# Two tables of routed sums instead of one in a mixture-of-experts stage on Trainium2

## The reference

```python
    x = x + gt1 * rmsnorm(mixed @ w_out[l], g_post_mix[l])
    h2 = modulate(rmsnorm(x, g_pre_ffn[l]), sh2, sc2)
    # moe: 8 of 64 experts per token, each swiglu(h, wg, wu, wd) of width 256
    routed = jax.ops.segment_sum(y_blocks.reshape(n_pad, d), tok_buf, num_segments=t + 1)[:t]
    y = routed + swiglu(h, w_sg, w_su, w_sd)
    x = x + gt2 * rmsnorm(y, g_post_ffn[l])
```

## Time and profile before

| | us |
|---|---|
| median of 3 runs | 2325.89 (2323.56 to 2327.89) |
| the profiled execution: its own time | 2333.98 |
| the profiled execution: span from first to last instruction | 2332.3 |
| attention, its first DMA | at 372.05 |
| experts, from the first to the last scatter | 1231.4 to 2271.5 |
| final | 2285.4 to 2332.3 |

### The profile page before, as it was taken

The page is one execution under the profiler, slowest core; times in us unless marked ns, Lnnn a source line. Parts: engine busy times, 40 slices in busy tenths (PEclk is TensorE's granted clock), DMA queues, the critical chain, the costliest instruction groups (busy, mean ns, idle before and its releaser), DMA issues. The chain is left out here.

```text
span 2332.3 us, 35734 instructions
## 1 busy us (share of the span) xinstructions
PE 2035.9 (87%) x9400; PEld 1452.3 (62%) x9401; DVE 1432.4 (61%) x2085; ACT 1278.9 (55%) x2004; POOL 869.0 (37%) x876
## 2 busy tenths in 40 slices
PE   4999995889888887899839999999999999999980
PEld 2776673655555554666427777777766777777760
DVE  3751564663358433455537777777676777777773
ACT  2421122556666565222127777776766777777761
POOL 1010103631155110044434455555444545544561
PEclk8999997899999998999969999999999999999995
DMA  6464436411221111343289998789999888789736
GB/s 248 140 190 118 130 115 187 114 32 39 44 48 39 39 35 63 133 92 101 56 255 293 317 336 247 231 233 328 336 330 331 260 232 229 203 258 334 202 61 233
DMA packets 284779, 420.25 MB, mean 180 GB/s; under 512 B 27233, under 2 KB 213345, under 8 KB 284689
## 3 DMA queue, kind: packets, MB, share of 16 engines
q1 hardware_dynamic: 213314, 281.25, 35.2%
q0 software_dynamic: 60496, 116.37, 22.6%
q10 hardware_dynamic: 10896, 21.71, 3.0%
HBM read 352.51 MB, written 91.54 MB: 190 GB/s over the span
## 5 line engine op out<-in xcount | busy, mean ns | idle before, releaser
L1802 DVE TENSOR_TENSOR w_gate_up_low<-w_gate_up,w_gate_up_high 128x1024 fp32r<-128x1024 f32 x318 | 378.2, 1217 | 15.9 <-ACT w_gate_up_high L1747 15.9
L1831 DVE TENSOR_TENSOR w_down_low<-w_down,w_down_high 128x2048 fp32r<-128x2048 f32 x104 | 238.4, 2292 | 161.5 <-ACT w_down_high L1771 161.5
L1747 ACT ACTIVATE w_gate_up_high<-w_gate_up 128x1024 fp32r x318 | 312.1, 1047 | 39.4 <-issue 28.6
L935 DVE TENSOR_REDUCE neg_max<-ps_scores 128x1 f32<-128x1280 f32 x128 | 190.3, 1490 | 223.6 <-PE ps_scores L1020 223.2
L1876 PE MATMUL ps_gu<-w_gate_up_high,gatheredT_high 128*128 128x512 f32 x630 | 256.1, 407 | 2.7 <-DVE gatheredT_low L1810 1.4
L1878 PE MATMUL ps_gu<-w_gate_up_high,gatheredT_low 128*128 128x512 f32 x630 | 248.7, 395 | 0.0
L1877 PE MATMUL ps_gu<-w_gate_up_low,gatheredT_high 128*128 128x512 f32 x630 | 248.6, 395 | 0.0
L1695 POOL DMA_INDIRECT gathered<-h_scratch,e_gather_index x108 | 195.6, 1811 | 96.5 <-POOL e_gather_index L1692 91.2
L1709 POOL DMA_INDIRECT y_scratch<-e_y,e_target_index x104 | 182.5, 1754 | 95.3 <-ACT e_y L1784 39.0
L1771 ACT ACTIVATE w_down_high<-w_down 128x2048 fp32r x104 | 199.6, 1919 | 29.2 <-issue 28.0
L1020 PE MATMUL ps_scores<-k_high_low,q_high 128*128 128x512 f32 (+1 forms) x384 | 167.5, 436 | 47.0 <-ACT probs L895 18.9
(11 more groups left out here) (257 smaller groups left out, 4328.9 us busy)
## 6 DMA issues: line engine op xcount, KB each, us to landing
w_gate_up<-in_w_exp_gate SPq DMA_DIRECT2D x64, 1024.0 KB, 10.4
w_gate_up<-in_w_exp_up SPq DMA_DIRECT2D x64, 1024.0 KB, 13.9
w_down<-in_w_exp_down SPq DMA_DIRECT2D x64, 1024.0 KB, 15.5
w_mod_later<-in_w_mod ACTq DMA_DIRECT2D x32, 512.0 KB, 3.8
w_mod_first<-in_w_mod SPq DMA_DIRECT2D x4, 2048.0 KB, 15.6
w_in_raw<-in_w_in SPq DMA_DIRECT2D x32, 256.0 KB, 3.9
k_high_low<-k_scratch POOLq DMA_DIRECT2D x10, 640.0 KB, 8.0
values<-in_tokens SPq DMA_DIRECT2D x10, 512.0 KB, 11.3
```

Source lines behind the costliest of these rows:

```text
L935: nc.vector.tensor_reduce(nm[:, n % 4:n % 4 + 1], S[:, span(u, r)], AX.X, ALU.max, negate=True).then_inc(s_m, 1)
L1747: act.activation(wH[:, 2 * j:2 * j + 2], wgu[:, ds(slot, 1), 2 * j:2 * j + 2].rearrange("p o k n -> p (o k) n"), ACT.Copy).then_inc(S["wH" ...
L1802: nc.vector.tensor_tensor(wL[:, 2 * j:2 * j + 2], wgu[:, ds(slot, 1), 2 * j:2 * j + 2].rearrange("p o k n -> p (o k) n"), wH[:, 2 * j:2 * ...
L1831: nc.vector.tensor_tensor(dl[:], wdn[:, ds(slot, 1)].rearrange("p o k n -> p (o k) n"), dh[:].bitcast(F32), ALU.subtract).then_inc(S["dl"], 1)
```

## The change

A second table of the same size is made, so that `y_d` is a list of two. Table 0 gets the shared expert's rows and the scatters of even blocks, table 1 those of odd blocks. The second table's 1024 token rows are filled with zeros by one DMA of 4 MB from DRAM to DRAM, which SP issues at the start of `attention` between two small loads. Each table's pad rows are zeroed by a DMA of 512 KB (before: two of 256 KB for the one table).

`scat` becomes two semaphores, one for each parity. POOL's wait ahead of the target copy and ACT's wait ahead of the refill both ask that the scatter two blocks ago, the last one on the same table, has landed.

In `final` ACT also loads table 1 (two DMAs of 2 MB, issued ahead of the 4 MB of residual rows), and DVE adds its tiles to those of table 0: two before its wait for the residual rows, the other six between the operations of its loop. ACT's squares wait for these sums. To have enough semaphores, `final` uses those of the expert weights again, from the value that they have reached.

```diff
@@ attention, SP
             sp.dma_start(slot_d, a["k_pads"]).then_inc(s_later, 16)
+            sp.dma_start(y2_d[0:SEQ, :], a["k_zeros"]).then_inc(s_later, 16)
             sp.dma_start(first_row[:], a["k_first"].broadcast_to([P, E])).then_inc(s_later, 16)
             sp.dma_start(token[:], a["k_token"]).then_inc(s_later, 16)
             sp.wait_ge(s_q[1], 64)
@@ output_and_router, SP
-                    sp.dma_start(y_d[(t - 2) * P:(t - 1) * P, :], yb[:]).then_inc(s_ys, 16)
+                    sp.dma_start(y_d[0][(t - 2) * P:(t - 1) * P, :], yb[:]).then_inc(s_ys, 16)
@@ experts
+        s_scat = [b.sem(ph, f"e_scattered{u}") for u in range(2)]
@@ experts, POOL, block n
-                pool.wait_ge(S["scat"], n * 16 + 32)
+                pool.wait_ge(s_scat[u], i * 16 + 16)
                 pool.sem_inc(S["carry"], 1)
                 nc.gpsimd.tensor_copy(si[u][:], ir[:, ds(n & (RING - 1), 1)]).then_inc(S["target"], 1)
-
+                pool.wait_ge(S["target"], n + 1)
                 pool.wait_ge(S["y"], n * 2 + 4)
-                pool.wait_ge(S["target"], n + 1)
                 pool.sem_inc(S["carry"], 1)
-                pool.indirect_dma_start(y_d, bass.IndirectOffsetOnAxis(ap=si[u][:, 0:1], axis=0), yb[u][:], None,
-                                        bounds_check=SEQ + P - 1, compute_op=ALU.add).then_inc(S["scat"], 16)
+                pool.indirect_dma_start(y_d[u], bass.IndirectOffsetOnAxis(ap=si[u][:, 0:1], axis=0), yb[u][:], None,
+                                        bounds_check=SEQ + P - 1, compute_op=ALU.add).then_inc(s_scat[u], 16)
@@ experts, POOL, before the loop
-            for h in range(2):
-                pool.dma_start(y_d[SEQ + h * HD:SEQ + (h + 1) * HD, :], zero[0:HD]).then_inc(S["scat"], 16)
+            for u in range(2):
+                pool.dma_start(y_d[u][SEQ:SEQ + P, :], zero[:]).then_inc(s_scat[u], 16)
@@ experts, ACT, block n
-                act.wait_ge(S["scat"], n * 16 + 16)
+                act.wait_ge(s_scat[u], i * 16 + 16)
@@ final, ACT
+            for h in range(2):
+                act.dma_start(y2[:, 4 * h:4 * h + 4], y_d[1][4 * h * P:(4 * h + 4) * P, :].rearrange("(t p) n -> p t n", p=P)).then_inc(s_y2[h], 16)
             act.dma_start(xt[:], x1_d.rearrange("(t p) n -> p t n", p=P)).then_inc(s_x, 16)
             for t in range(NT):
-                act.wait_ge(s_y[t // 2], 16)
+                act.wait_ge(s_sum, t + 1)
@@ final, DVE
+            def joined(t):
+                dve.wait_ge(s_y[t // 2], y_base[t // 2] + 16)
+                dve.wait_ge(s_y2[t // 4], 16)
+                nc.vector.tensor_tensor(yt[:, t], yt[:, t], y2[:, t], ALU.add).then_inc(s_sum, 1)
+
+            joined(0)
+            joined(1)
             dve.wait_ge(s_x, 32)
             for t in range(NT):
+                if t + 2 < NT:
+                    joined(t + 2)
                 dve.wait_ge(s_rs, 2 * t + 2)
```

More of the change, by code:

```diff
@@ L677, in _, with attention @@
                     mod_products(wl[:, i % 2], h * QK, QK, h < 2, h >= 2, s_mm)
-def attention(b, a, ident, rows, nlam, mhalf, moe, wa, vv, q_d, k_d, o_d, rows_d, slot_d):
+def attention(b, a, ident, rows, nlam, mhalf, moe, wa, vv, q_d, k_d, o_d, rows_d, slot_d, y2_d):
     nc = b.nc
@@ L813, in _ @@
             store(NU - 1)
-            sp.wait_ge(s_later, 80)
+            sp.wait_ge(s_later, 96)
             sp.wait_ge(s_before, 16)
@@ L1641, in experts @@
             "xT", "xH", "xL", "wH", "wL", "wused", "gu", "silu", "act", "aTp", "aH", "dh", "dl",
-            "dn", "y", "weight", "rows", "target", "scat", "landed", "carry", "zeroed")}
+            "dn", "y", "weight", "rows", "target", "landed", "carry", "zeroed")}
         s_gather = [b.sem(ph, f"e_gathered{u}") for u in range(2)]
+        s_scat = [b.sem(ph, f"e_scattered{u}") for u in range(2)]
         s_index = [b.sem(ph, f"e_index_loaded{u}") for u in range(2)]
@@ L1734, in _ @@
                 pool.wait_ge(s_index[u], turns * 16 + 48)
-            pool.wait_ge(S["scat"], turns * 32 + 32)
+            for u in range(2):
+                pool.wait_ge(s_scat[u], turns * 16 + 16)
         @block.scalar
@@ L1915, in _, with final @@
             blocks(pe, body)
-def final(b, a, rows_d, mhalf, x1_d, y_d, out):
+def final(b, a, rows_d, mhalf, s_w, x1_d, y_d, out):
     nc = b.nc
@@ L1923, in final @@
         xt = b.sb(ph, "x1_tiles", [P, NT, D])
+        y2 = b.sb(ph, "y_tiles_odd", [P, NT, D])
         g2 = b.sb(ph, "gain_row", [P, D])
@@ L1926, in final @@
         ms = b.sb(ph, "f_mean", [P, 3, NT])
-        s_y = [b.sem(ph, f"y_loaded{h}") for h in range(NT // 2)]
+        s_y = s_w[0:NT // 2]
+        y_base = [(E - h + WS - 1) // WS * 48 for h in range(NT // 2)]
         s_x = b.sem(ph, "x1_loaded")
+        s_y2 = [b.sem(ph, f"y_odd_loaded{h}") for h in range(2)]
+        s_sum = b.sem(ph, "f_sum")
         s_sq = b.sem(ph, "f_sq")
@@ L1938, in _ @@
             for h in range(NT // 2):
-                sp.dma_start(yt[:, 2 * h:2 * h + 2], y_d[2 * h * P:(2 * h + 2) * P, :].rearrange("(t p) n -> p t n", p=P)).then_inc(s_y[h], 16)
+                sp.dma_start(yt[:, 2 * h:2 * h + 2], y_d[0][2 * h * P:(2 * h + 2) * P, :].rearrange("(t p) n -> p t n", p=P)).then_inc(s_y[h], 16)
             for t in range(NT):
@@ L1983, in program @@
     h2_d = nc.dram_tensor("h2_scratch", [SEQ, D + E], F32).ap()
-    y_d = nc.dram_tensor("y_scratch", [SEQ + P, D], F32).ap()
+    y_d = [nc.dram_tensor(f"y_scratch{u}", [SEQ + P, D], F32).ap() for u in range(2)]
     rows_d = nc.dram_tensor("rows_scratch", [1, 4 * D], F32).ap()
@@ L1995, in program @@
         s_slots = [b.sem(top, f"slots_stored{u}") for u in range(2)]
+        s_w = [b.sem(top, f"e_weights_loaded{u}") for u in range(WS)]
         with ExitStack() as kv:
@@ L2002, in program @@
             wa = b.sb(kv, "w_out_ahead", [P, AHEAD, D])
-            attention(b, a, ident, rows, nlam, mhalf, moe, wa, vv, q_d, k_d, o_d, rows_d, slot_d)
+            attention(b, a, ident, rows, nlam, mhalf, moe, wa, vv, q_d, k_d, o_d, rows_d, slot_d, y_d[1])
             output_and_router(b, a, ident, rows, mhalf, moe, wa, p8, s_slots, o_d, x1_d, h2_d, y_d, slot_d)
@@ L2008, in program @@
             wdn = b.sb(ex, "w_down", [P, WS, 2, D])
-            s_w = [b.sem(ex, f"e_weights_loaded{u}") for u in range(WS)]
             routing_tables(b, a, ident, mask, total, tab, wgu, wdn, s_w, p8, token, s_slots, slot_d)
             experts(b, a, ident, tab, wgu, wdn, s_w, s_slots, h2_d, y_d, slot_d)
-        final(b, a, rows_d, mhalf, x1_d, y_d, out)
+        final(b, a, rows_d, mhalf, s_w, x1_d, y_d, out)
 def rope_table():
@@ L2042 @@
     host["k_steps"] = np.arange(WS, E, WS, dtype=np.float32)[None, :(E - 1) // WS]
+    host["k_zeros"] = np.zeros((SEQ, D), np.float32)
     host["k_first"] = (np.arange(E, dtype=np.float32) * SEQ + 1)[None, :]
```

## The result

Twelve runs of each kernel side by side gave 2332.59 us for the changed one (2326.18 to 2339.39) and 2326.61 us for the one before (2318.79 to 2330.63). The ratio is 1.0029, with a 95% interval of 1.0016 to 1.0043: 6.7 us slower, between 3.7 and 10.0 (the medians themselves lie 6.0 apart). A second call, in the experiments, gave 1.0014 (1.0001 to 1.0026), that is 3.3 us (5.8 between the medians). I had forecast 3.9 us less. The kernel moved the other way, if only by 0.1 to 0.3%. One run of the whole study, 2456.97 us in the last experiment at a granted clock of 0.83 instead of 0.96, was in a slower state and is left out of every median.

A forecast was written before the change was run, and what follows sets the result against it. PE, busy 87% of the span, was taken as the bound, held up in the loop by a closed chain of scatters. Terms -27.9 - 0.8 + 7.4 + 17.4 = -3.9 us took 2325.9 to 2322.0 us; range 2310 to 2336.

The forecast's parts named there:

- loop, first to last silu: Experts' loop: waiting for the scatter two blocks back gives 27.9 us of the 39.1 lost above 9.70 per block.
- gap behind the last silu: Loop's end: the last target copy no longer waits 0.80 us for a landing scatter, 0.8 us less.
- zeros at attention's start: Attention's start: the 4.19 MB fill shares the engines with K and Q half and half, delaying everything by 7.4 us.
- end: Final stage: residual rows land 10.0 us later behind table 1, and six additions take 7.4 us; 17.4 in all.
- the fill goes first: Attention's start: a bound on the zeros' cost, with the fill served ahead of K and Q at 419 GB/s, 10.0 us.
- my own signs of being wrong: ACT waits for weights early, third window returns most of 14 us, scatter over 13 us, or fill's cost at either bound.
- rival (b): Loop: two scatters in flight make weights late; third and fourth window give nothing, +9.2 us, 2335.1 us; chance 0.12.
- third window: Loop stretch of one-block experts, bound by DMA at 1.03: of 14.0 us lost, 2.8 come back; bounds 0 and 14.0.
- fourth window: Loop stretch followed by experts of three and four blocks, whose loads aren't needed soon: all 10.3 us lost are gained.
- rival (d): Loop: scatter latency grows past 13 us and the wait returns; half the gain gone, +10.1 us, 2336.0 us; chance 0.08.
- (a): Loop: all waits go, weights' lead and DMA engines suffice; 39.1 us gained, sum -15.1, 2310.8 us; chance 0.15.
- Rival (c): Attention's start: zeros hidden, or cost 10 or 20 us; 2314.6, 2324.6 or 2334.6 us; chance hidden 0.08, at 20 us 0.07.

The follow-up runs named there:

- the last experiment: The kernel before, with one table, its residual rows loaded in four parts so that DVE starts with the first pair; 2320.93 us, ratio 0.9967.

## Why the prediction was wrong

The sum, term by term; measured is the difference of the means over all profiles with and without the part in question:

| term | forecast | measured |
|---|---|---|
| loop, first to last silu | -27.9 | -25.0 (1023.9 of seven, 1048.9 of six) |
| gap behind the last silu | -0.8 | -0.7 (20.7 of eight, 21.4 of six; it wanders by 1.6) |
| zeros at attention's start | +7.4 | +12.1 (24.67 of three, 12.54 of ten) |
| end | +17.4 | +16.9 (10.1 + 6.8) |
| sum | -3.9 | +3.3 |

3.3 us lies in the interval of the second comparison (0.2 to 6.0) and just under that of the first (3.7 to 10.0). The runs of the parts by themselves, each beside the kernel before, give -24.9 for the loop, +13.5 for the end and +10.5 for the fill, -0.9 together. From their three intervals I estimate some 9 us either way for that sum, so it contradicts nothing and is too coarse to confirm; the sum rests on the stages.

**The step that failed is the fill's: "if both queues get half of the engines, that takes about 7.4 us more".** It is the term +7.4, and it measured 12.1. The place was right, and that the fill takes the engines from K and Q; how they share was not. I shared time by queues. The engines shared it by turns, packet for packet (50 against 52), and a packet of the fill was 64 KB where one of K and Q was 1.7 KB. The fill in 2 KB pieces shows that this is the cause: 62.1% for K and Q instead of 10.8%, and 2.5 us instead of 12.1. The fill even came out 2 us above my bound of 10.0 for "the fill goes first". That bound took the rate of 419 GB/s from the earlier trace rows; the 64 packets of the fill needed 13.05 us for their 4.19 MB, which is 321 GB/s. Why this copy inside DRAM ran slower stays open; a reading and a writing of each byte in full, my 20.0, it was not. The 4.7 us of this term take the sum of -3.9 past zero. That the fill's cost comes out at a bound was one of my own signs of being wrong.

Here the Trainium skill (DMA: Bandwidth & Descriptors, Queues, rings and completion order) would have done better than I did. It says that a DMA engine takes its queues in turn and finishes a whole packet before it goes on to the next. I had set it aside under rival (b) because of q0's 0.5% of the earlier trace rows. At attention's start the trace agrees with it, with 50 packets of q1 and 52 of q0 side by side. And I misread: the scatter issued at 1698.38 has its first packet of row data at 1703.38, 5.0 us later, and the window ends ahead of that. From 1703 to 1708 us of the kernel before both queues move:

```profile
q0 software_dynamic: 193, 0.60, 56.7%
q1 hardware_dynamic: 318, 0.88, 47.9%
```

So the 0.5% showed a scatter that hadn't begun, not one that weights kept out. Why it begins 5.0 us behind its issue under weight loads, and 2.25 us behind it without them (the one at 2225.04), stays open.

**The loop fell 2.9 us short, and the windows came out otherwise than forecast.** What they lose above 9.70 us for a block, as means over the six profiles without the change and the seven with it, cut at the same blocks:

| window of the earlier trace rows | without | with | gain | forecast |
|---|---|---|---|---|
| first | 8.4 (7.3 to 10.0) | 0.0 | 8.4 | 8.5 |
| second | 1.9 (0.6 to 3.4) | 0.0 | 1.9 | 3.3 |
| third | 15.8 (14.0 to 16.9) | 13.3 (12.2 to 14.4) | 2.5 | 2.8 |
| fourth | 7.4 (5.5 to 10.3) | 1.6 (0.2 to 3.3) | 5.9 | 10.3 |
| fifth | 6.3 (3.0 to 8.3) | 0.0 | 6.3 | 3.0 |

The third window gave its 2.8 almost, although the first pair of profiles shows 0.5. The term that was too large is the fourth window's. I took its 10.3 from the one execution in which it lost most, and 1.6 of what it loses stays with the change; the fifth, at 3.0 the least of six, made good for some of it.

In the third window I had read the bound correctly: the DMA share stayed at 1.03 and the first idle time is ACT's ahead of the weight copy. In the profiled execution what I had counted as slack, the 4.3 us by which the weights were early at the window's end, is gone by its eighth block. ACT in that stretch, then SP:

```profile
1634.21 2.96 ACT L1749 ACTIVATE w_gate_up_high<-w_gate_up 128x1024 fp32r x3 [2.09 <-SPq L1665]
...
1647.86 2.95 ACT L1749 ACTIVATE w_gate_up_high<-w_gate_up 128x1024 fp32r x3 [6.22 <-SPq L1665]
```

```profile
1634.70 3.13 SPq L1516 DMA_DIRECT2D w_gate_up<-in_w_exp_gate  x1
1637.88 5.98 SPq L1517 DMA_DIRECT2D w_gate_up<-in_w_exp_up  x1
1643.90 3.70 SPq L1518 DMA_DIRECT2D w_down<-in_w_exp_down  x1
```

ACT starts 0.26 us after SP's third issue ends at 1647.60, which looks like a matter of order. But these weights had landed only at 1646.85, 0.75 us earlier, and the kernel with the earlier signal gained nothing in sum; the lighter loads confirmed capacity. With two thirds of a window at 9.70 and the rest in a few stalls of 2 to 6 us, the sum over seventeen blocks is still the DMA engines' time. In the profiled execution the loop gained 27.0, of which 1.6 are the first block's and not the change's. Over seven executions it is 25.0; in the slowest of them the dense blocks lost 17.8 us.

**What held.** A closed chain of scatters set the period: with the wait moved two blocks back it is gone, and four windows of the changed kernel stand at or near 9.70. That the first pair of profiles gives 8.5, 3.3, 10.1 and 3.0 where the working had 8.5, 3.3, 10.3 and 3.0 is no more than that: the same execution of the kernel before is subtracted in both. The fourth window did gain, 5.9 of its 7.4 us, although the weights stream there at a DMA share of 1.05. Scatters landed within 12.2 us (12.7 in the slowest profile of the others), under the 13 that were covered, so rival (d) didn't come. Nor did (a): the third window kept 13.3 us of loss. Of rival (b) there is the order of things, waits for weights in the third window, but not the price: it had both windows gain nothing, and they gained 8.4. Rival (c) is the one that came: the fill at 10 us or a little above. Had I taken that bound, the forecast would have been 2324.6; with the loop's shortfall it is some 2327.5, or 1.6 us more than before, inside the second comparison's interval and under the first's. The chances for a faster kernel add up to 0.43, where I had written 0.42.

The end cost 16.9 for 17.4: landing 10.1 for 10.0, additions 6.8 for 7.4. Each of the six adds 1.14 us and not its full length of 1.225: in the trace of the kernel before, L1970 starts at 2323.19 us and the operation behind it at 2324.33, before its end. By the Trainium skill's figure of some 358 GB/s for a core (DMA: Bandwidth & Descriptors, Specifications) the landing would have been 11.7 later; the trace doesn't agree, and the measured rate of the earlier trace rows was the right one to take.

Carrying the sum to the median of the runs was sound. What misleads is the reverse: a single profile on either side, whose untouched stages differ by as much as the whole effect. My prices by window were such a reading too.

## What to carry to other kernels

A copy that nobody waits for still takes its turns: how much it takes from the transfers that somebody does wait for depends on the bytes of one packet of it against one packet of theirs, here at two sizes. Give it small pieces or a place where no one waits. And when a change buys a long stage with something at the seams, cost the seams as carefully as the stage: here 25 us were won in the loop and 29 paid for outside it, of which 12 by moving one line and some 12 more by ordering the end's loads could be had back (9 of these the kernel with one table can have too).

## What the runs showed of the hardware

**A stall costs PE twice.** PE alone in slices of 2 us behind the wait of 6.22 us in the changed kernel (busy and count, granted clock, DMA share, GB/s):

```profile
1650.00:1652.00 2.00, 0.28 (x2) 1.00 1.07 240
1652.00:1654.00 2.00, 0.73 (x4) 0.94 1.01 332
1654.00:1656.00 2.00, 2.00 (x6) 0.50 1.05 407
1656.00:1658.00 2.00, 2.00 (x8) 0.71 1.06 384
1658.00:1660.00 2.00, 2.00 (x9) 1.00 1.09 389
```

PE was busy for 1.0 of the 4 us ahead of 1654, and then worked for more than 2 us at a granted clock of 0.50, the 1.2 GHz level, before it came back to 2.4 GHz. Six multiplications instead of eight or nine fit into such a slice. That is 2 x (1 - 0.50) + 2 x (1 - 0.71) = 1.6 us lost on top of the wait, by my estimate. Behind the stall of 5.40 us at 1721.83 the clock stood at 0.50 again, from 1725.5 to 1732.2 us; behind the one of 2.09 us it didn't fall. ACT's next weight copies in turn waited for PE (1.05, 0.88 and 0.33 us; with 1.14 and 0.38 behind the next stall these are the 3.8 us for PE in L1749's row).

**The share of a queue follows the size of its packets.** Two queues with work moved as many packets as each other: 50 and 52 with 64 KB against 1.7 KB, for 89.2% and 2.8% of the engines; 735 and 724 with 2.1 KB against 3.0 KB, for 47.4% and 61.7%. All at the same place, with the same bytes to move.

**A scatter's first data comes late.** 5.0 us behind the issue under weight loads, 2.25 us without them, of 9.5 and 6.4 us until it has landed.
